# The mixing stage of a hybrid encoder layer, from tiles of 128 tokens to blocks of 384 tokens

## The chip, the core and the metric

The kernel runs on one core of a Trainium2 chip. The metric is the device time of one execution in microseconds (us). Engines are named as in the profile: PE (TensorE) multiplies matrices and transposes, DVE (VectorE), ACT (ScalarE) and POOL (GpSimd) do elementwise work, SP (SyncE) issues most transfers. PSUM is the memory that PE writes, SBUF the one that all engines read.

## The reference

One layer over 2048 prompt tokens and 64 sample tokens with 1024 channels. In short:

```python
mod = silu(c) @ w_ada + b_ada                     # sh1, sc1, g1, sh2, sc2, g2
h = x * (1 + sc1) + sh1
proj = h @ w_in                                   # q 512, k 128, v 128, a 512, g 512 columns
attn = sink_attention(q, k, v, bias, sinks)       # 8 heads, 2 kv heads, a window of 128 tokens and the own chunk
u = a * sigmoid(g)
y = depthwise_conv(u, w_dw, 31 taps) + b_dw       # 512 channels, causal
conv = silu(layer_norm(y))
mix = concat([attn, conv]) @ w_out
x1 = layer_norm(ALPHA * x + (1 + g1) * mix)
h2 = x1 * (1 + sc2) + sh2                         # goes on to a mixture of experts: 16 experts, 2 per token
```

The outputs are y for both sequences and the last keys, values and convolution inputs of each.

## The kernel before

Four stages follow one another, with a barrier between: `setup` (modulation vectors, weights split in two half-precision parts), `mix` (all of the above up to h2 and the router's logits), `route` with `experts`, and `finish`. The change is in `mix`, with small parts of `setup`.

`mix` works in 17 tiles: tile 0 holds the 64 sample tokens, tiles 1 to 16 hold 128 prompt tokens each. Every engine has its own program, written by hand, and runs it in order; engines meet at semaphores only. A step of the loop holds four tiles at different ages: the next tile's x (lag -1), projections of tile j0, attention and taps of j1, layer norm of the convolution and output projection of j2, residual and second modulation of j3. Steps 4 to 15 run in a hardware loop of two steps.

- Projections (L1110): tokens lie on PE's output partitions. For each of four jobs (q, k with v, g, a) 24 matmuls stream up to 512 columns of `w_in` past a stationary slice of `hT` (three products of half-precision parts, eight slices of 128 channels). The results lie token by token, so q, k and the gated input u are turned by PE transposes (`turn_in`, L1093) and copied by ACT.
- Modulation of x: two POOL operations over 1024 columns (L721, L723), then PE transposes, an ACT cast (L921) and a DVE subtraction (L1082) for the two parts of `hT`.
- Taps (L965): 31 taps over four channel groups, 124 DVE operations of 128 columns a tile, which read `uT` and add to `y`, both in SBUF. They are put between DVE's other work at fixed cuts (`TAP_CUTS`).
- Attention: scores in four rounds of two heads (L1124), DVE adds the bias and takes row maxima (L981), ACT takes exponentials head by head (L871), PE transposes them (p), ACT copies (L902), PE multiplies with v (L1184), ACT scales (L931), PE transposes (o).
- Convolution's norm: PE transposes y, DVE statistics (L991), POOL's power (L730), a DVE shift (L1002), ACT (L814), PE transposes back (z), ACT (L833, L837), DVE (L1033), ACT and POOL for the two parts.
- Output projection (48 matmuls of 512 columns), ACT copies (L806), POOL gate and residual (L740, L743), DVE statistics (L1017), shift (L1028), ACT normalizes (L848), POOL (L757 to L765), PE transposes h2, ACT copies (L887), router logits (L1168).

Of the kernel before, what the change touches and what calls it, by code (L numbers as in the profile page):

```python
# [20 lines left out]
F32 = mybir.dt.float32  # L21
# [6 lines left out]
P = 128  # L28
# [108 lines left out]
def build(nc, a):  # L137
# [3 lines left out]
    vec_rows = nc.dram_tensor("vec_rows", [6, 2, D], F32)  # L141
    bias_rows = nc.dram_tensor("bias_rows", [HEADS, NREL], F32)

    with ExitStack() as keep:
# [16 lines left out]
        with ExitStack() as mixer:  # L161
            def held(name, shape, dt=F32):
# [12 lines left out]
                "kT": held("kT", [P, 2, 2 * P]),  # L175
                "kv": held("kv", [P, 2, 2 * P]),
                "vprev": held("vprev", [P, 2, P]),
                "uT": held("uT", [P, 2, CB, HIST + P]),
# [33 lines left out]
def setup(nc, a, K, M, vec_rows, bias_rows):  # L212
    with ExitStack() as ctx:
# [23 lines left out]
        vec = sb("vec", [P, 6, 2, KD])  # L237
        onesc = sb("onesc", [P, 2, KD])
        vec_row = sb("vec_row", [96, P])
# [43 lines left out]

        pieces = [(a["w_in"][0, k * P:(k + 1) * P, :], [w[:, k, :] for w in M["w_in"]], INW) for k in range(KD)]
        pieces += [(a["w_out"][0, k * P:(k + 1) * P, :], [w[:, k, :] for w in M["w_out"]], D) for k in range(KD)]

        with nc.Block() as block:
# [22 lines left out]
            def _(pool):  # L310
# [7 lines left out]
                pool.memset(M["uT"][:, 1, :, 0:HIST], 0.0).then_inc(zeroed, 1)  # L318
# [8 lines left out]
            def _(act):  # L327
                for dst, src in ((dw_rows[:], a["w_dw"][0]), (cache_k[:], a["cache_attn_k"].rearrange("l b t h d -> (l b t) (h d)")),
# [3 lines left out]
                                 (M["vprev"][:, 0, :], a["cache_attn_v"].rearrange("l b t h d -> (l b t) (h d)"))):  # L332
# [19 lines left out]
                act.copy(M["kT"][:, 0, 0:P], ps_u[:, 0, :]).then_inc(history_ready, 1)  # L352
                act.wait_ge(history_turned, 2)
                act.copy(M["uT"][:, 0, :, 0:HIST], ps_b[:, 0:CB * HIST].rearrange("p (c t) -> p c t", c=CB)).then_inc(history_ready, 1)
                act.wait_ge(dw_turned, 1)
                act.copy(M["w_dw"][:], ps_t[:, :, 0:TAPS]).then_inc(dw_ready, 1)
# [10 lines left out]
                for i, (_, (hi, _), cols) in enumerate(pieces):  # L367
                    act.wait_ge(raw_loaded[i % RAW_RING], 16 * (i // RAW_RING + 1))
                    act.activation(hi, raw[:, i % RAW_RING, :cols], ACT.Copy, scale=W_SCALE).then_inc(hi_ready, 1)
# [6 lines left out]
                act.copy(vec_row[:], ps_v[0:96, :]).then_inc(vec_row_ready, 1)  # L376
# [7 lines left out]
            def _(pe):  # L384
# [41 lines left out]
                pe.transpose(ps_v[0:96, :], vec[:].rearrange("p v s k -> p (v s k)"), K["ident"][:]).then_inc(vec_turned, 1)  # L426

            @block.vector
            def _(dve):
# [9 lines left out]
                for c in range(ADA_CHUNKS):  # L439

                    while split < min(len(pieces), SPLITS_PER_CHUNK * (c - 2)):
                        _, (hi, lo), cols = pieces[split]
                        dve.wait_ge(hi_ready, split + 1)
                        dve.scalar_tensor_tensor(lo, raw[:, split % RAW_RING, :cols], W_SCALE, hi, ALU.mult, ALU.subtract).then_inc(lo_ready, 1)
# [13 lines left out]
                dve.tensor_scalar(vec[:, 0], part(1), 1.0, None, ALU.add).then_inc(vec_ready, 1)  # L458
                dve.tensor_copy(vec[:, 1], part(0)).then_inc(vec_ready, 1)
                dve.tensor_scalar(vec[:, 2], part(2), 1.0, 1.0 / (ALPHA * W_SCALE), ALU.add, ALU.mult).then_inc(vec_ready, 1)  # L460
                dve.tensor_scalar(vec[:, 5], part(5), 1.0, 1.0 / ALPHA, ALU.add, ALU.mult).then_inc(vec_ready, 1)
                dve.tensor_scalar(onesc[:], part(4), 1.0, None, ALU.add).then_inc(vec_ready, 1)
                dve.wait_ge(vec_ready, 5)
                dve.tensor_tensor(vec[:, 3], onesc[:], col(LN1_G), ALU.mult).then_inc(vec_ready, 1)
                dve.tensor_tensor(vec[:, 4], onesc[:], col(LN1_B), ALU.mult).then_inc(vec_ready, 1)
                dve.wait_ge(vec_ready, 7)
                dve.tensor_tensor(vec[:, 4], vec[:, 4], part(3), ALU.add).then_inc(vec_ready, 1)
# [8 lines left out]
TURNS = [("y", 0, 2), ("z", 0, 2), ("q", 0, 0), ("k", 0, 0), ("h2", 0, 3), ("h2", 1, 3),  # L476
         ("p", 0, 1), ("p", 1, 1), ("p", 2, 1), ("p", 3, 1), ("u", 0, 0), ("x", 0, -1), ("x", 1, -1), ("o", 0, 1)]

OUTPUTS = [("lg", 0, 3), ("pv", 0, 1), ("out", 0, 2), ("out", 1, 2)]


def before(ring, i, name, n):

    at = [(x, y) for x, y, _ in ring].index((name, n))
    m, c = i
    while True:
        at -= 2
        if at < 0:
            at += len(ring)
            c -= 1  # L490
            if isinstance(m, int) and c < -1:
                return None
        what, number, lag = ring[at]
        j = lagged((m, c), lag)
        if j is not None:
            return what, number, j


def mix(nc, a, K, M, vec_rows, hidden2, normed1):
    with ExitStack() as ctx:  # L500
# [7 lines left out]
        x_h = sb("x_h", [P, 2, D])  # L508
        x_res = sb("x_res", [P, D])
        rows = sb("rows", [P, 5, D])  # L510
        ln1_rows = sb("ln1_rows", [P, 2, D])
        hT = [sb(f"hT_{part}", [P, KD, P], F16) for part in ("hi", "lo")]
        q_tok = sb("q_tok", [P, AW])
        gate = sb("gate", [P, CH])
        qT = sb("qT", [P, 2, GROUP, P])
        y = sb("y", [P, 2, CB, P])
        probs = sb("probs", [P, HEADS, 2 * P])
        pT = sb("pT", [P, 2, 2, 2, P])
        o_tok = sb("o_tok", [P, AW])
        mixT = [sb(f"mixT_{part}", [P, KD, P], F16) for part in ("hi", "lo")]  # L520
# [4 lines left out]
        u_out = sb("u_out", [P, CH])  # L525
# [3 lines left out]
        h2T = sb("h2T", [P, KD, P])  # L529
        row_max = sb("row_max", [P, HEADS])  # L530
# [15 lines left out]
        score = [ctx.enter_context(nc.psum_tensor(f"score{n}", [P, 2, 2 * P], F32)) for n in range(2)]  # L546
        outp = [ctx.enter_context(nc.psum_tensor(f"outp{n}", [P, 512], F32)) for n in range(2)]


        x_loaded = [sem(f"x_loaded{n}") for n in range(2)]  # L550
# [1409 lines left out]
```

## Time and profile before

| | |
|---|---|
| time, median of three runs | 1859.59 us (1857.54 to 1860.09) |
| span of the profiled execution | 1858.3 us |
| what the median has beside the span | 1.3 us |
| mixing stage, first x load to the first load of the next stage | 121.7 to 1167.1 us |
| DVE, PE, ACT, POOL busy, share of the span | 84%, 80%, 43%, 31% |
| mean granted TensorE clock | 0.876 |

The span runs from the first to the last instruction of the profiled execution; all positions are us from its start. A clock of 1.00 is 2.4 GHz and 0.50 is 1.2 GHz. The shares are over all four stages, so what binds the mixing stage is to be read in windows of that stage.

### The profile page before, as it was taken

The page shows a single profiled execution, that of the slowest core. Times are in us where ns is not written, and L with a number is a line of the kernel's source. Part 1 is how long each engine was busy: PE and PEld are TensorE (multiplying, and loading weights), DVE is VectorE, ACT ScalarE, POOL GpSimd, SP SyncE. Part 2 cuts the span into 40 slices and gives each one's busy share as a digit, 9 for nine tenths or more (in the row PEclk, how much of TensorE's full clock was granted, in tenths as well). Part 3 has the DMA queues.
Part 4 walks back from the last instruction along what each step waited for, and adds up shares of the span by engine and source line. Part 5 has one row for each costly group of instructions (what it writes and reads, how often), then busy time and mean ns, then how long its engine had stood idle before and what let it go on. Part 6 is the DMA issues. An engine that isn't in the chain of part 4 may idle for free. (4 is left out here: it accounts for less than half of the span.)

```text
span 1858.3 us, 26059 instructions
## 1 busy us (share of the span) xinstructions
PE 1479.8 (80%) x7082; PEld 819.7 (44%) x7082; DVE 1555.3 (84%) x3420; ACT 802.2 (43%) x1429; POOL 582.9 (31%) x422
## 2 busy tenths in 40 slices
PE   5958988778887888878988864369999999995664
PEld 1214545445454554545545442335554555552221
DVE  1415899999999999999999970769999999993887
ACT  1302332333323333233332331058888888882332
POOL 0012132344323443234432335011222222213775
PEclk9978889889988898888988866579999999997777
DMA  9961011011000110001100001856899333324774
GB/s 325 400 212 39 12 49 32 35 47 46 24 33 34 46 46 23 35 34 46 46 23 23 28 35 45 283 161 239 288 322 385 113 111 107 110 101 152 227 231 153
DMA packets 90720, 218.28 MB, mean 117 GB/s; under 512 B 8034, under 2 KB 42758, under 8 KB 88591
## 3 DMA queue, kind: packets, MB, share of 16 engines
q1 hardware_dynamic: 65554, 136.25, 21.0%
q0 software_dynamic: 11808, 43.00, 7.2%
q10 hardware_dynamic: 13277, 38.20, 5.4%
q14 instruction: 61, 0.50, 0.1%
q8 instruction: 20, 0.33, 0.1%
HBM read 165.90 MB, written 51.56 MB: 117 GB/s over the span
## 5 line engine op out<-in xcount | busy, mean ns | idle before, releaser
L965 DVE SCALAR_TENSOR_TENSOR y<-uT,w_dw_cols,y 128x128 f32<-128x128 f32 (+1 forms) x2040 | 738.8, 437 | 0.7
L1655 DVE SCALAR_TENSOR_TENSOR w_gate_up_lo<-w_gate_up_ring,w_gate_up_hi 128x2048 f16<-128x2048 f16 x96 | 219.4, 2287 | 25.3 <-ACT w_gate_up_hi L1580 24.9
L1580 ACT ACTIVATE w_gate_up_hi<-w_gate_up_ring 128x2048 f16 x96 | 182.8, 1906 | 59.5 <-SPq L1538 40.1
L1100 PE MATMUL proj<-w_in_hi,hT_hi 128*128 128x512 f16 (+3 forms) x544 | 200.9, 369 | 1.1 <-DVE hT_lo L1082 1.1
L1100 PE MATMUL proj<-w_in_lo,hT_hi 128*128 128x512 f16 (+3 forms) x544 | 199.7, 367 | 0.0
L1100 PE MATMUL proj<-w_in_hi,hT_lo 128*128 128x512 f16 (+3 forms) x544 | 198.7, 365 | 0.0
L730 POOL TENSOR_TENSOR y_small<-y_small,mhalf 128x1 f32<-128x1 f32 (+1 forms) x17 | 9.3, 549 | 515.3 <-DVE y_small L996 515.3
L1698 PE MATMUL ps_up<-w_gate_up_hi,slot_rowsT_hi 128*128 128x512 f16 x384 | 147.0, 383 | 18.9 <-DVE slot_rowsT_lo L1680 14.0
L1561 POOL COPY slot_index<-slot_token 128x1 int32 (+1 forms) x48 | 44.8, 934 | 351.5 <-PE eturn L1719 308.4
L1698 PE MATMUL ps_up<-w_gate_up_lo,slot_rowsT_hi 128*128 128x512 f16 x384 | 146.6, 382 | 0.0
L1698 PE MATMUL ps_up<-w_gate_up_hi,slot_rowsT_lo 128*128 128x512 f16 x384 | 146.6, 382 | 0.0
L1100 PE MATMUL outp<-w_out_hi,mixT_hi 128*128 128x512 f16 (+1 forms) x272 | 111.3, 409 | 2.5 <-DVE logits L1068 2.5
L1686 DVE SCALAR_TENSOR_TENSOR w_down_lo<-w_down_ring,w_down_hi 128x2048 f16<-128x2048 f16 x48 | 109.6, 2284 | 3.3 <-ACT w_down_hi L1631 2.5
L1100 PE MATMUL outp<-w_out_lo,mixT_hi 128*128 128x512 f16 (+1 forms) x272 | 109.7, 403 | 0.0
L1100 PE MATMUL outp<-w_out_hi,mixT_lo 128*128 128x512 f16 (+1 forms) x272 | 108.5, 399 | 0.0
L1922 PE MATMUL ps_v<-x,ident 128*128 128x512 f32 (+1 forms) x68 | 57.0, 934 | 50.7 <-ACT y_rows L1869 46.9
L1093 PE MATMUL turn<-ident,gate 128*128 128x128 f32 (+1 forms) x68 | 18.3, 422 | 96.8 <-DVE gate L1063 96.8
L1631 ACT ACTIVATE w_down_hi<-w_down_ring 128x2048 f16 x48 | 91.7, 1911 | 5.8 <-issue 3.8
L418 PE MATMUL ps_mod<-w_ada_ring,c_silu 128*2 128x512 f32 x192 | 87.4, 610 | 8.6 <-DVE c_silu L433 4.3
L902 ACT COPY pT<-turn 128x512 f32<-128x512 f32 x60 | 33.8, 587 | 128.5 <-PE turn L1093 128.5
L1093 PE MATMUL turn<-ident,h 128*128 128x128 f32 (+1 forms) x136 | 27.2, 366 | 74.9 <-POOL h L759 74.9
L871 ACT ACTIVATE probs<-probs,nmax 128x256 f32<-128x256 f32 (+2 forms) x136 | 65.9, 485 | 39.0 <-DVE nmax L1044 39.0
(254 smaller groups left out, 3118.1 us busy)
## 6 DMA issues: line engine op xcount, KB each, us to landing
w_ada_ring<-in_w_ada SPq DMA_DIRECT2D x12, 2048.0 KB, 15.0
expert_rows<-out_rows ACTq DMA_DIRECT2D x48, 512.0 KB
w_gate_up_ring<-in_w_gate SPq DMA_DIRECT2D x16, 1024.0 KB
w_gate_up_ring<-in_w_up SPq DMA_DIRECT2D x16, 1024.0 KB
w_down_ring<-in_w_down SPq DMA_DIRECT2D x16, 1024.0 KB
x_h<-in_x_prompt SPq DMA_DIRECT2D x16, 512.0 KB
x_res<-in_x_prompt SPq DMA_DIRECT2D x16, 512.0 KB, 3.3
hidden<-h SPq DMA_DIRECT2D x16, 512.0 KB, 2.6
```

The costliest lines, as they stand in the source:

```text
L418: mm = pe.matmul(ps_mod[c % 2][:], c_silu[:, k:16:KD], w_ada[:, c % ADA_RING, k, :], start=(k == 0), stop=(k == KD - 1))
L871: act.activation(probs[:n, h, lo:hi], probs[:n, h, lo:hi], ACT.Exp, bias=nmax[:n, h:h + 1], accum_out=prob_sum[:n, h:h + 1]).then_inc(prob ...
L965: dve.scalar_tensor_tensor(y[:, p, c, :n], u, w, y[:, p, c, :n], ALU.mult, ALU.add).then_inc(taps_done, 1)
L1093: mm = pe.transpose(bank[:nf, place, :np_], src, ident[:np_, :np_])
L1100: mm = pe.matmul(out, x[xp][:, k, :n], w[wp][:, k, cols], start=(k == 0 and wp == xp), stop=(k == KD - 1 and xp == 1))
L1561: pool.tensor_copy(index[:, c:c + 1], K["slot_token"][:, tile_at(j)]).then_inc(index_ready, 1)
L1580: act.activation(gate_up_parts[0][:, at, k:k + KD // 2, :, :].rearrange("p k a n -> p (k a n)"), w_gate_up[:, bass.ds(b, 1), k:k + KD // 2 ...
L1631: act.activation(down_parts[0][:, c, :, :].rearrange("p k n -> p (k n)"), w_down[:, bass.ds(b, 1), :, :].rearrange("p b k n -> p (b k n)") ...
L1655: dve.scalar_tensor_tensor(flat[1], w_gate_up[:, bass.ds(b, 1), k, :, :].rearrange("p b k a n -> p (b k a n)"), W_SCALE, flat[0], ALU.mult ...
L1686: dve.scalar_tensor_tensor(flat[1], w_down[:, bass.ds(b, 1), :, :].rearrange("p b k n -> p (b k n)"), W_SCALE, flat[0], ALU.mult, ALU.subt ...
L1698: mm = pe.matmul(out, x, w, start=(k == 0 and xp == wp), stop=(k == blocks - 1 and xp == 1))
L1922: pe.matmul(ps_v[p][h][:n, :], ident[:n, :n], x1[:n, p, cols], start=True, stop=False)
```

## The change

The 17 tiles are grouped in six blocks: tiles 0 to 2 (64 + 128 + 128 tokens), four blocks of three tiles (384 tokens), and tiles 15 and 16. The loop is over phases p; the code is written out in full (no hardware loop). Phase p projects block p, and then makes up to three steps: in each, tile i of block p goes through attention (`mine`), tile i of block p-1 through output projection and residual (`leaves`), tile i+1 of block p-1 through the convolution's norm (`then`), tile i-1 of block p-1 through h2 and logits (`last`), and tile i of block p+1 through modulation and transposes (`nxt`).

- Projections: the weight slice is stationary and `hT` streams, up to 384 columns. q, k, g and a come out by channels, 13 jobs of 24 matmuls; v keeps tokens on partitions (24 matmuls of 128 columns a tile). The transposes of q, k and u go, and their copies. The score banks and the projection banks are the same two.
- Modulation: `x_part` on ACT reads the transposed x in PSUM and applies scale and shift per channel, four operations of 128 columns for each half, then a cast; DVE subtracts (`x_low`). POOL's two operations go.
- Taps: one operation covers the block's 350, 384 or 256 columns and adds up in PSUM (`tap_sum`), two channel groups in turn; the last tap writes `y` to SBUF. 744 operations in all, against 2108.
- Scores: two rounds of four heads. Exponentials of four heads, then of the other four.
- `gate` also holds the modulated x, and `y_tok` also holds the attention's output.

```diff
+BLOCKS = [[0, 1, 2], [3, 4, 5], [6, 7, 8], [9, 10, 11], [12, 13, 14], [15, 16]]
+JOBS = ["k", "q0", "q1", "q2", "q3", "v", "g0", "a0", "g1", "a1", "g2", "a2", "g3", "a3"]
...
+                def x_part(t, h):
...
+                    for c in range(4):
+                        k = 4 * h + c
+                        last = act.activation(h32[:, c, :n], turn_bank("x", t, h)[:, c, :n], ACT.Identity,
+                                              scale=M["mod_in"][:, 0, seq_of(t), k:k + 1], bias=M["mod_in"][:, 1, seq_of(t), k:k + 1])
+                    last.then_inc(h32_ready, 1)
+                    act.wait_ge(h32_ready, 2 * t + h + 1)
+                    act.copy(hT[0][:, 4 * h:4 * h + 4, at:at + n], h32[:, :, :n]).then_inc(hT_hi_ready, 1)
...
+                        u, w = U[:, c, k:k + n], M["w_dw"][:, c, k:k + 1]
...
+                            dve.wait_ge(taps_done, TAP_OPS * b + m - 1)
...
+                            to = y[:, c, 0:n] if k == TAPS - 1 else tap_sum[e][:, 0:n]
+                            dve.scalar_tensor_tensor(to, u, w, tap_sum[e][:, 0:n], ALU.mult, ALU.add).then_inc(taps_done, 1)
...
+                        at = {"k": K0, "q": Q0, "a": A0, "g": G0}[job[0]] + (int(job[1]) * P if len(job) == 2 else 0)
+                        for k in range(KD):
+                            for xp, wp in ((0, 0), (1, 0), (0, 1)):
+                                mm = pe.matmul(bank[:, 0:size(b)], M["w_in"][wp][:, k, at:at + P], hT[xp][:, k, 0:size(b)],
+                                               start=(k == 0 and xp == wp), stop=(k == KD - 1 and wp == 1))
...
+                        if mine is not None:
+                            scores(mine, 0)
+                        if then is not None:
+                            y_turn(then)
+                        if leaves is not None:
+                            out_project(leaves, 0)
+                        if then is not None:
+                            z_turn(then)
+                        if mine is not None:
+                            scores(mine, 1)
+                        if leaves is not None:
+                            out_project(leaves, 1)
+                        if last is not None:
+                            h2_turn(last)
+                        if mine is not None:
+                            prob_turn(mine, 0)
+                        if last is not None:
+                            logits(last)
...
+                        if mine is not None:
+                            attend(mine, 3)
+                            o_turn(mine)
```

ACT's order in a step is: norm of y (`then`), first half of the output copy (`leaves`), gain of the convolution (`then`), exponentials of four heads, high part of the convolution, second output copy, the other four exponentials, h2 copies (`last`), two copies of probabilities, `x_part` of the first half (`nxt`), two copies of probabilities, `x_part` of the second half, the residual's norm (`leaves`), the scaling of the attention's output (`mine`), its high part. On DVE the shift for the residual's norm stands behind `x_low` of the second half.

How the order moves shows best at two places. The first is PE in the middle of a step. `turn` are the transposes (probs: probabilities, o_tok or y_tok: the attention's output, x_h: the next x), `outp<-kv,pT` or `outp<-v,pT` the product with the values, and the router's logits stand ahead of it. Before, at the join of two steps of the loop:

```order
L1100 MATMUL outp<-w_out_hi,mixT_lo 128x512
L632 REGISTER_ALU
L1093 MATMUL turn<-ident,o_tok 128x128 x4
L1093 MATMUL turn<-ident,y 128x128 x4
L1118 REGISTER_ALU
L1124 MATMUL score<-kT,qT 128x256 x4
```

After, from the logits of one tile to the scores of the next:

```order
L1445 MATMUL outp<-w_router,h2T 128x20 x8
L1348 MATMUL turn<-ident,probs 128x128 x4
L1464 MATMUL outp<-v,pT 128x64 x4
L1348 MATMUL turn<-ident,x_h 128x128 x4
L1348 MATMUL turn<-ident,probs 128x128 x4
L1464 MATMUL outp<-v,pT 128x64 x4
L1348 MATMUL turn<-ident,probs 128x128 x4
L1464 MATMUL outp<-v,pT 128x64 x4
L1348 MATMUL turn<-ident,x_h 128x128 x4
L1464 MATMUL outp<-v,pT 128x64 x4
L1348 MATMUL turn<-ident,y_tok 128x128 x4
L1407 MATMUL proj<-kT,qT 128x256 x4
```

The transposes of the attention's output stood behind the output projection of another tile (48 matmuls); now they stand directly behind the attention that they belong to, and the scores of the next tile behind them.

The second place is DVE where one phase ends and the next begins. Before, the gated input of a tile (`gate<-gate,proj`) came between taps of 128 columns:

```order
L965 SCALAR_TENSOR_TENSOR y<-uT,w_dw_cols,y 128x128
L1061 REGISTER_ALU
L1062 REGISTER_ALU
L1063 SCALAR_TENSOR_TENSOR gate<-gate,proj 128x512
L1068 ISA
L1068 TENSOR_TENSOR logits<-outp,b_router 128x20
L964 REGISTER_ALU
L965 SCALAR_TENSOR_TENSOR y<-uT,w_dw_cols,y 128x128
```

After, from the last operation of a phase (`oT_lo`) to the next block's gated input (`uT<-gate,proj`):

```order
L1241 TENSOR_TENSOR oT_lo<-turn,oT_hi 128x512
L1155 SCALAR_TENSOR_TENSOR tap_sum<-uT,w_dw_cols,tap_sum 128x384 x9
L1262 TENSOR_TENSOR logits<-outp,b_router 128x20
L1155 SCALAR_TENSOR_TENSOR tap_sum<-uT,w_dw_cols,tap_sum 128x384 x38
L1155 SCALAR_TENSOR_TENSOR y<-uT,w_dw_cols,tap_sum 128x384 x2
L1165 COPY uT<-uT 128x2x30
L1173 SCALAR_TENSOR_TENSOR uT<-gate,proj 128x384
L1185 BN_STATS y_stat<-turn 128x6
```

Nine taps, the logits of the tile that leaves last, and 40 more taps stand ahead of the next block's first gated input and of the transposes of y.

## Rows read from the trace of the kernel before

**Rows 1.** Windows view, the loop's steps: length, then busy us and instructions by engine
```profile
core 0: us, PE busy (x) PEld busy (x) DVE busy (x) ACT busy (x) POOL busy (x), PEclk, DMA share, GB/s
211.00:1111.00 900.00, 737.58 (x3984) 461.43 (x3981) 874.07 (x2497) 301.88 (x829) 333.22 (x195) 0.89 0.10 35
```
**Rows 2.** Timeline of POOL, the power, once a tile: start us, duration us, engine
```profile
604.30 0.55 POOL L730 TENSOR_TENSOR y_small<-y_small,mhalf 128x1 f32<-128x1 f32 x1 [29.25 <-DVE y_small L996]
...
720.89 0.55 POOL L730 TENSOR_TENSOR y_small<-y_small,mhalf 128x1 f32<-128x1 f32 x1 [29.25 <-DVE y_small L996]
```
**Rows 3.** Timelines of DVE and POOL: taps alone and beside POOL, operations beside POOL
```profile
202.12 9.53 DVE L965 SCALAR_TENSOR_TENSOR y<-uT,w_dw_cols,y 128x128 f32<-128x128 f32 x36
...
604.81 2.49 POOL L740 TENSOR_TENSOR v<-v,rows 128x512 f32<-128x512 f32 x2
605.09 1.01 DVE L1002 SCALAR_TENSOR_TENSOR y_small<-y_aggr,y_small 128x1 f32<-128x1 f32 x1
606.02 0.68 DVE L1007 TENSOR_TENSOR mixT_lo<-turn,mixT_hi 128x512 f16<-128x512 f32 x1
...
619.43 2.35 POOL L759 TENSOR_TENSOR h<-h,rows 128x1024 f32<-128x1024 f32 x1
619.50 18.94 DVE L965 SCALAR_TENSOR_TENSOR y<-uT,w_dw_cols,y 128x128 f32<-128x128 f32 x28
```
**Rows 4.** Timeline of DVE: taps of 64 columns, operations of 512 columns
```profile
180.47 5.56 DVE L965 SCALAR_TENSOR_TENSOR y<-uT,w_dw_cols,y 128x64 f32<-128x64 f32 x28
...
614.35 0.68 DVE L1033 SCALAR_TENSOR_TENSOR conv<-y_tok,conv 128x512 f32<-128x512 f32 x1
...
643.06 0.68 DVE L1063 SCALAR_TENSOR_TENSOR gate<-gate,proj 128x512 f32<-128x512 f32 x1
```
**Rows 5.** Timeline of PE at full clock, one tile
```profile
601.77 1.99 PE L1124 MATMUL score<-kT,qT 64*128 64x256 f32 x8
...
605.00 0.38 PE L1100 MATMUL proj<-w_in_hi,hT_hi 128*128 128x512 f16 x1
605.21 0.38 PE L1100 MATMUL proj<-w_in_lo,hT_hi 128*128 128x512 f16 x1
...
629.63 1.86 PE L1168 MATMUL outp<-w_router,h2T 128*128 128x20 f32 x16
631.34 1.07 PE L1093 MATMUL turn<-ident,probs 128*128 128x128 f32 x8
...
634.20 0.39 PE L1184 MATMUL outp<-kv,pT 128*128 128x64 f32 x2
634.42 0.39 PE L1184 MATMUL outp<-vprev,pT 128*128 128x64 f32 x2
```
**Rows 6.** Timeline of ACT, one tile; the last row by groups: busy us, mean ns
```profile
609.58 1.50 ACT L833 ACTIVATE conv<-turn,cols 128x128 f32<-128x128 f32 x4
...
614.60 1.24 ACT L848 ACTIVATE n<-v,l_small 128x1024 f32<-128x1024 f32 x1 [2.08 <-DVE l_small L1028]
...
623.93 1.04 ACT L887 COPY h2T<-turn 128x512 f32<-128x512 f32 x2
...
647.24 1.75 ACT L931 ACTIVATE o_tok<-outp,rden 128x64 f32<-128x64 f32 x8
...
L871 ACT ACTIVATE probs<-probs,nmax 128x256 f32<-128x256 f32 x120 | 59.3, 495 | 37.1 <-DVE nmax L1044 37.1
```
**Rows 7.** Groups of DVE by line and form: busy us, mean ns
```profile
L981 DVE CUSTOM_DVE_ANT_0 probs<-score,bias 128x256 f32<-128x256 f32 x120 | 44.5, 416 | 3.5 <-issue 3.3
...
L1017 DVE BATCH_NORM_STATS2 l_stat<-v 128x6 f32<-128x512 f32 x32 | 20.4, 676 | 20.8 <-POOL v L743 20.8
```
**Rows 8.** Windows view, PE alone: length, busy us, granted clock
```profile
619.90:621.90 2.00, 0.06 (x1) 1.00 0.00 0
622.90:626.20 3.30, 3.30 (x10) 0.50 0.31 127
637.30:643.80 6.50, 0.00 (x1) 0.70 0.00 1
```
**Rows 9.** Timeline of SP: the first load of the mixing stage, the next stage's first
```profile
121.73 0.58 SPq L654 DMA_DIRECT2D x_h<-in_x_sample  x1
...
1167.10 0.66 SPq L1227 DMA_DIRECT2D w_gate_up_ring<-in_w_gate  x1
```

More of the change, by code:

```diff
@@ L470, in setup @@
         nc.clear_and_free_semaphores(sems)
         nc.all_engine_barrier()
[L476 to L496, printed above, removed]
+BLOCKS = [[0, 1, 2], [3, 4, 5], [6, 7, 8], [9, 10, 11], [12, 13, 14], [15, 16]]
@@ new lines, with out_order @@
+TURNS = turn_order()
+TURN_AT = {use: n for n, use in enumerate(TURNS)}
+def out_order():
+    order = []
+    for p in range(NB + 1):
+        if left_from(p) is not None:
+            order.append(("lg", left_from(p), 0))
+        for i in range(steps_of(p)):
+            mine, leaves, last = (tile_in(*x) for x in ((p, i), (p - 1, i), (p - 1, i - 1)))
+            if leaves is not None:
+                order += [("out", leaves, 0), ("out", leaves, 1)]
+            if last is not None:
+                order.append(("lg", last, 0))
+            if mine is not None:
+                order.append(("pv", mine, 1))
+    order.append(("lg", BLOCKS[-1][-1], 0))
+    return order
@@ new lines, in o_high @@
+                def o_high(t):
+                    n, b, i = width(t), BLOCK_OF[t], BLOCKS[BLOCK_OF[t]].index(t)
+                    act.wait_ge(o_turned, t + 1)
+                    older = tile_in(b - 1, i)
+                    if older is not None:
+                        act.wait_ge(out_done, 2 * older + 2)
+                    act.copy(oT[0][:, i, :, :n], turn_bank("o", t)[:, :, :n]).then_inc(oT_hi_ready, 1)
+                for t in BLOCKS[0]:
+                    for h in range(2):
+                        x_part(t, h)
@@ new lines, in wait_bank, with x_turn @@
+                def wait_bank(name, t, n):
+                    use = next(banks)
+                    assert use == (name, t, n), (use, name, t, n)
+                    if held[n] is not None:
+                        what, t_, n_ = held[n]
+                        s, value = out_read[what]
+                        pe.wait_ge(s, value(t_, n_))
+                    held[n] = use
+                def x_turn(t, h):
+                    n = width(t)
+                    pe.wait_ge(x_loaded, 16 * t + 16)
+                    turn_in("x", t, h, [(c, x_h[:n, (4 * h + c) * P:(4 * h + c + 1) * P], n, P) for c in range(4)], x_turned)
@@ L1216, in _, with h2_turn @@
-                over_steps(pe, step, first=-1)
+                            x = oT[xp][:, i, k, :n] if k < CB else convT[xp][:, t % 2, k - CB, :n]
+                            mm = pe.matmul(outp[h][:n, :], x, M["w_out"][wp][:, k, h * 512:(h + 1) * 512],
+                                           start=(k == 0 and xp == wp), stop=(k == KD - 1 and xp == 1))
+                    mm.then_inc(out_done, 1)
+                def h2_turn(t):
+                    n = width(t)
+                    pe.wait_ge(h2_ready, 2 * t + 2)
+                    for h in range(2):
+                        turn_in("h2", t, h, [(c, h2[:n, (4 * h + c) * P:(4 * h + c + 1) * P], n, P) for c in range(4)], h2_turned)
@@ L1219, in load_expert @@
+                h2_turn(BLOCKS[-1][-1])
+                logits(BLOCKS[-1][-1])
+                k_turn(BLOCKS[-1][-1])
+                state_turn(1)
 def load_expert(sp, a, W, e, b):
```

1309 lines of the change are left out of this document (757 added, 552 removed).

## The prediction

> **What bounds the kernel now.** First the windows of the mixing stage: in 900 us of its steps DVE is busy 874, PE 738, ACT 302, POOL 333 [rows 1]. DVE has no room, so its work sets the period, which POOL's once-a-tile power shows: 116.6 us for two tiles, 58.3 a tile, 174.9 for three [rows 2]. Then DVE's timeline says why. 36 taps that nothing disturbs take 9.53 us, 0.264 each; 28 taps beside POOL's long operations take 18.94, 0.676 each [rows 3]. A DVE operation that reads two SBUF tensors waits for POOL: the shift L1002, over one column, took 1.01 us, and ended when POOL's first half of L740 did; L1007, with one input in PSUM, ran beside POOL in 0.68 [rows 3]. Of 58.3 us a tile, 124 taps take 33 undisturbed and some 11 are lost beside POOL. PE's own work is less, so it waits for DVE, and its clock falls after each wait [rows 8].
>
> **What the change takes away.** 2108 taps become 744. From 64 to 128 columns a tap grows from 0.199 (5.56 by 28) to 0.264 [rows 3, 4], 1.02 ns a column, so 384 columns make 0.264 + 256 x 0.00102 = 0.525 us, and 256 make 0.395. No row shows DVE writing PSUM. The bounds are 0.39 (384 columns at that slope, no start-up) and 0.80 (a tap that lasts as long as a 512-column operation, 0.68, with the start-up of 0.13 that is left of a tap of 64 columns); I take 0.525, since a 512-column operation takes 0.68 with both inputs in SBUF and 0.68 with one in PSUM [rows 4]. The Trainium skill ("VectorE: DVE Perf Modes", section on the TRN2 errata) gives an operation from PSUM 62 cycles more than one from SBUF; by that a tap would be 0.59 and the whole 13 us longer. The two rows of 0.68 show no such difference, and the sum goes by them. The new taps have one SBUF input and so should not wait for POOL, as L1007 did not. Per block of three tiles DVE's taps fall from 3 x 44 = 132 us to 124 x 0.525 = 65. That takes DVE off the end of the chain. So the question is what is late next.
>
> **What is late next: the order inside a step.** PE runs in order. In a step it waits at the transposes of the attention's output for ACT, and only then starts the next tile's scores. Head and tail of a tile's attention therefore lie behind one another, where before another tile's output projection lay between. I follow the middle step of a block, at full clock, from the scores of its tile (time 0):
>
> Head: scores 2.0 [rows 5], y transposes 0.5, 24 matmuls of 0.215 = 5.2 [rows 5], to 7.7. DVE meanwhile: row maxima 4 x 0.37 = 1.5 [rows 7], statistics 1.3, two taps; its shift waits for POOL's multiply as L1002 did, to 7.9. ACT's norm 0.8, z transposes to 9.6, second scores to 11.6, row maxima and their maximum to 13.8.
> Tail: four exponentials of 0.494 (59.3 by 120) [rows 6] to 15.8, convolution cast 0.5; the second output projection ends at 16.8, its copy at 17.5; four exponentials and the sink to 19.6; two h2 copies 1.04 [rows 6] to 20.7; logits 1.86 [rows 5] to 22.7; probabilities' transposes 0.55, values 4 matmuls 0.9, x transposes 0.55 [rows 5] to 24.7; `x_part` 1.50 (as L833) + 0.1 + 0.6 = 2.2 [rows 6] to 27.0; two copies to 28.1, values and x transposes to 29.3; second `x_part` to 31.5; DVE's `x_low` 0.7 and shift 0.2, because the shift stands behind it, to 32.5; residual's norm 1.24 to 33.7; eight scalings 1.75 [rows 6] to 35.5; transposes to 36.1.
> POOL is not last here (residual done at 22.7, statistics of 2 x 0.64 [rows 7] at 24.4). The first step has no h2 and logits, 33.3; the third no y and z, 33.9. Together 103.3 us, of which PE works about 26 a step.
>
> **Projections.** A job is 24 x 0.215 x 384/512 = 3.87 us [rows 5]. Thirteen make 50.3. v's 72 matmuls of 128 columns are bounded by 0.054 (their columns alone) and 0.116 (a weight load and a short matmul, as the logits: 1.86 by 16 [rows 5]); I take 0.116, 8.4. Transposes and logits of the leaving tile make 4.0. The logits come after four jobs and the h2 transposes, at 18.5; 40 taps stand behind them on DVE, 21.0, to 39.7, and only then can PE turn y, which it reaches at 38.5. Another 0.6 for the last gated input. Sum 64.5 us.
>
> **Clock.** After 1.94 us of idle PE the granted clock was 0.50 from 622.9 to 626.2 though PE was busy, and it had fallen within 6.5 idle us [rows 8]. A stretch of 3.3 us at half clock costs 1.7. I put 1.7 on each of the three 5 us waits at the ends of steps, and half of it on the three shorter ones: 7.6 a block.
>
> A block of three tiles is 64.5 + 103.3 + 7.6 = 175.4, against 174.9 now. Steady state gains nothing.
>
> **The ends.** The stage lasts 1045.4 us now [rows 9]. After: first phase 140 (an estimate: three loads with `x_part` and `x_low`, 24; projection of 320 columns 50; three steps without another tile's work, 23, 20 and 23); block 1 171 (no logits beside its projections); blocks 2 to 4 3 x 175.4 = 526; the last block, 256 columns, 53 + 65 = 118; then 112 in which little overlaps (tile 14's residual and logits 32, 40 taps of 0.395 16, norm of tile 15 10, output projection 12, residual 10, POOL's modulation and residual of tile 16 15, norm and POOL's four operations 14, store 3); barrier 3. Sum 1070, 24 more than now. The transposes that go (nine of 53 a tile) and POOL's two operations are not on this path. Setup's split of `w_in` into more pieces lies beside the loads of `w_ada` there; if it doesn't, under 3 us. The later stages are the same. The sum is against the profiled execution, 1858.3 of span; the median has 1.3 beside that, which I keep. Forecast: 1859.6 + 24 = **1883 us**, for itself 1860 to 1910.
>
> **Rivals.**
> 1. The clock holds. PE's waits are shorter than I reckon, or fall so that the clock stays at 1.00. Then 7.6 a block and some in the ends go, 42 in all: 1841. For it: the dense projections; against: [rows 8], where 1.94 us of idle was enough. This is the rival on the other side; it decides once less than half of the clock's charge comes.
> 2. Scores overlap. In each new round consecutive score matmuls use different halves of the partitions, before the same half. If two of them run side by side, a round is 1.0 instead of 2.0 [rows 5] and 2 us go from each of some 14 full steps: 1855. The Trainium skill ("TensorEngine Tiling (Array Packing)", Tiling Modes) says that separate row tiles work in parallel, up to twice as fast. No run here shows it.
> 3. Taps are dear. At 0.80 DVE's 40 taps end 11 later in each of five phases, and the taps inside a step hold the second row maxima by 1 to 2: 1883 + 55 + 20 = 1958; at 0.66 half of that, 1920.
> 4. The waits hide one another and a step is PE's 26 us. Then 25 a block go: 1765. Against it stands the one order of PE, in which nothing lies behind the output's transposes.
>
> **How the numbers follow.** Chances: forecast 0.50, clock 0.17, scores 0.13, taps 0.14, PE-bound 0.06. About 0.2% (3.7 us) is what a measurement of this kernel can tell from no change. Faster comes from the clock (0.14 of 0.17), half of the scores' case (0.07), PE-bound (0.06) and the forecast's edge (0.06): 0.33; no change 0.08; slower 0.59. The range for 8 in 10 is 1825 to 1925: it takes in both clock cases and a tap of 0.66, and leaves out the PE-bound case and the dearest taps.
>
> **What would show it.** Right: in the new trace DVE is busy under 75% of the mixing stage; taps of 384 columns start 0.50 to 0.56 apart, also beside POOL; a step lasts 33 to 40 us; PE waits 4 to 6 us for the scaling of the attention's output at the end of each; ACT is busy nearly throughout the last 20 us of a step; the clock shows 0.50 at the start of steps. Wrong: steps under 31 us, or DVE busy throughout, or taps above 0.65, or a stage whose third block is far from 175 us.

## The result and the profile after

The changed kernel takes 1866.29 us (median of five runs, 1864.19 to 1866.97) against 1859.55 for the kernel before in the same session: 1.0038 of it, 95% interval 1.0025 to 1.0050. It is slower by 6.7 us, where 24 were forecast. The direction came out; the size of the change does not fit, so a term of the sum is wrong, and the experiments look for it.

The page of the profiled execution, its span and its busy times:

```profile
span 1863.6 us, 23581 instructions
PE 1454.6 (78%) x7587; PEld 856.5 (46%) x7587; DVE 1175.0 (63%) x2093; ACT 833.0 (45%) x1512; POOL 484.7 (26%) x388
```

DVE was 84% busy and is 63%; PE and ACT hardly moved. The windows view by phases answers to [rows 1] (length, then busy us and instructions of PE, weight loads, DVE, ACT and POOL, the granted clock, DMA):

```profile
121.30:270.50 149.20, 94.15 (x618) 69.77 (x619) 57.04 (x157) 51.33 (x167) 0.00 (x0) 0.69 0.14 44
270.50:436.20 165.70, 141.79 (x830) 94.96 (x828) 94.64 (x231) 61.71 (x167) 42.38 (x31) 0.84 0.10 32
...
609.20:779.90 170.70, 139.97 (x854) 93.19 (x852) 96.85 (x232) 63.61 (x169) 49.78 (x34) 0.88 0.10 38
...
947.90:1064.10 116.20, 95.28 (x666) 74.43 (x664) 69.59 (x182) 38.22 (x103) 33.20 (x25) 0.85 0.09 33
```

A full block takes 170.7 us where three tiles took 174.9 [rows 2], with DVE busy 97 of them. So the steady state did gain 4 us a block; the ends lost more. The stage lasts from 121.34 to 1175.56, 1054.2 us against 1045.4 [rows 9].

Timelines of DVE and of POOL beside it (start us, us, engine, line; x is the count) answer to [rows 3]:

```profile
629.00 20.04 DVE L1155 SCALAR_TENSOR_TENSOR tap_sum<-uT,w_dw_cols,tap_sum 128x384 f32<-128x384 f32 x38
715.25 2.34 POOL L863 TENSOR_TENSOR n<-n,rows 128x1024 f32<-128x1024 f32 x1
715.62 1.99 DVE L1195 SCALAR_TENSOR_TENSOR y_small<-y_aggr,y_small 128x1 f32<-128x1 f32 x1
717.53 2.71 DVE L1155 SCALAR_TENSOR_TENSOR tap_sum<-uT,w_dw_cols,tap_sum 128x384 f32<-128x384 f32 x5
717.67 2.36 POOL L865 TENSOR_TENSOR n<-n,rows 128x1024 f32<-128x1024 f32 x1
```

38 taps take 20.04, 0.527 each; five beside POOL's L865 take 2.71, 0.54 each (a tap's own record is 0.62 long and overlaps the next one, which weighs more in a group of five). No tap of the whole kernel has a record of over 0.623. L1195, over one column with both inputs in SBUF, begins beside POOL's L863 and ends with it, after 1.99 us. The taps, which now have one input in PSUM, are not held up by POOL, as the prediction reckoned from L1007.

PE's middle step of that block, from one tile's transposes of the attention's output (`turn<-ident,y_tok`) to the next tile's (in brackets the wait and its releaser), answers to [rows 5]:

```profile
708.64 1.11 PE L1348 MATMUL turn<-ident,y_tok 128*128 128x128 f32 x4 [4.35 <-ACT y_tok L1050]
709.69 2.08 PE L1407 MATMUL proj<-kT,qT 64*128 64x256 f32 x8
...
719.24 1.13 PE L1407 MATMUL proj<-kT,qT 64*128 64x256 f32 x8
...
728.97 0.63 PE L1348 MATMUL turn<-ident,probs 128*128 128x128 f32 x4 [2.43 <-ACT h2T L1017]
729.43 1.89 PE L1445 MATMUL outp<-w_router,h2T 128*128 128x20 f32 x16
...
744.61 1.12 PE L1348 MATMUL turn<-ident,y_tok 128*128 128x128 f32 x4 [5.11 <-ACT y_tok L1050]
```

The step is 36.0 us long (708.64 to 744.61), as forecast at full clock (36.1), but not in the way it was forecast: the second round of scores takes 1.13 us, not 2.0. The first takes 2.08, at half clock. The windows view of PE alone, around the start of that step (length, busy, clock), answers to [rows 8]:

```profile
704.30:708.60 4.30, 0.00 (x0) 0.50 0.26 101
708.60:714.40 5.80, 5.76 (x21) 0.50 0.22 90
714.40:718.70 4.30, 4.30 (x21) 0.99 0.00 2
```

Behind the wait of 4.35 us the clock stays at 0.50 through 5.8 us of work; the 3.3 us of [rows 8] stood behind 1.9 us of idle. It did not fall in that wait, though: it shows 0.50 from the wait's first microsecond. The fall came earlier in the step, while PE worked, some 2 us behind a shorter wait of 2.34 us. PE's timeline, and the windows view with the columns of the phases above:

```profile
695.60 1.10 PE L1464 MATMUL outp<-v,pT 128*128 128x64 f32 x8 [2.34 <-ACT pT L1027]
```

```profile
690.00:695.00 5.00, 3.26 (x20) 1.81 (x17) 2.93 (x6) 4.16 (x18) 3.34 (x3) 1.00 0.00 0
695.00:700.00 5.00, 4.40 (x29) 4.21 (x29) 2.04 (x7) 3.63 (x9) 3.05 (x4) 0.74 0.24 66
700.00:705.00 5.00, 4.30 (x21) 4.11 (x20) 1.61 (x4) 2.71 (x6) 0.21 (x1) 0.50 0.33 112
```

The view of PE's waits over the mixing stage (us, times, the longest):

```profile
PE turn L1348 <- ACT y_tok L1050: 67.0, 17, 5.1
PE turn L1348 <- DVE y L1155: 27.3, 4, 10.7
PE turn L1348 <- ACT h2T L1017: 21.9, 9, 2.5
PE outp L1464 <- ACT pT L1027: 15.0, 11, 2.3
```

The first row is the wait at the ends of steps. The second is the wait of the transposes of y for the 40 taps that stand behind the logits; another 16 us of the same kind lie in the drain.

### The profile page after: what moved, and what is told of

Its sections match the earlier page's. It is cut to its first block and busy times, and to the rows that moved or that the text cites. A ratio compares the mean times of both kernels' runs of the same rounds, so it can differ in the third digit from the quotient of the medians.

```text
span 1863.6 us, 23581 instructions
## 1 busy us (share of the span) xinstructions
PE 1454.6 (78%) x7587; PEld 856.5 (46%) x7587; DVE 1175.0 (63%) x2093; ACT 833.0 (45%) x1512; POOL 484.7 (26%) x388
## 5 line engine op out<-in xcount | busy, mean ns | idle before, releaser
L1155 DVE SCALAR_TENSOR_TENSOR tap_sum<-uT,w_dw_cols,tap_sum 128x384 f32<-128x384 f32 (+2 forms) x696 | 356.0, 589 | 0.0
L1918 ACT ACTIVATE w_gate_up_hi<-w_gate_up_ring 128x2048 f16 x96 | 182.8, 1906 | 59.9 <-SPq L1876 40.1
L1391 PE MATMUL proj<-hT_hi,w_in_hi 128*128 128x384 f16 (+2 forms) x624 | 201.8, 323 | 5.5 <-DVE hT_lo L1180 5.5
L1391 PE MATMUL proj<-hT_lo,w_in_hi 128*128 128x384 f16 (+2 forms) x624 | 201.2, 322 | 0.0
L1391 PE MATMUL proj<-hT_hi,w_in_lo 128*128 128x384 f16 (+2 forms) x624 | 201.1, 322 | 0.0
L1464 PE MATMUL outp<-v,pT 128*128 128x64 f32 (+2 forms) x528 | 99.4, 351 | 17.9 <-ACT pT L1027 15.0
L1464 PEld LDWEIGHTS outp<-v,pT 128*128 128x128 f32 (+2 forms) x528 | 94.9, 268 | 24.5 <-ACT pT L1027 18.4
L1180 DVE TENSOR_TENSOR hT_lo<-gate,hT_hi 128x512 f16<-128x512 f32 (+1 forms) x34 | 22.9, 672 | 111.1 <-ACT hT_hi L909 111.1
L1348 PE MATMUL turn<-ident,y_tok 128*128 128x128 f32 (+1 forms) x136 | 29.0, 352 | 76.8 <-ACT y_tok L1050 67.0
L1247 DVE BATCH_NORM_STATS2 l_stat<-v 128x6 f32<-128x512 f32 (+1 forms) x34 | 21.9, 685 | 99.8 <-POOL v L839 99.8
L1348 PE MATMUL turn<-ident,probs 128*128 128x128 f32 (+2 forms) x264 | 54.4, 348 | 36.0 <-ACT h2T L1017 21.9
```

The source lines that it names most:

```text
L1155: dve.scalar_tensor_tensor(to, u, w, tap_sum[e][:, 0:n], ALU.mult, ALU.add).then_inc(taps_done, 1)
L1348: mm = pe.transpose(bank[:nf, at, :np_], src, ident[:np_, :np_])
L1391: mm = pe.matmul(bank[:, 0:size(b)], M["w_in"][wp][:, k, at:at + P], hT[xp][:, k, 0:size(b)], start=(k == 0 and xp == wp), stop=(k == KD - ...
L1464: mm = pe.matmul(outp[1][:n, h * HD:(h + 1) * HD], pT[:nk, f % 2, e, kt, :n], V[:nk, slot, s * HD:(s + 1) * HD], start=(x == 0), stop=(x = ...
L1918: act.activation(gate_up_parts[0][:, at, k:k + KD // 2, :, :].rearrange("p k a n -> p (k a n)"), w_gate_up[:, bass.ds(b, 1), k:k + KD // 2 ...
```

## The experiments

Every time is a median beside the kernel before on the same chip (1859.4 to 1860.3 there). "The changed kernel" is 1866.3.

### Is a round of scores short because its matmuls alternate halves?

```diff
-                    for e in range(2):
-                        for s in range(KV):
+                    for s in range(KV):
+                        for e in range(2):
```

> The four score matmuls of a round go in pairs on the same half of the partitions instead of alternating halves; nothing else changes. Theory A (two consecutive score matmuls on different halves run side by side, and the forecast priced them one behind the other): a round grows from 1.07 to 2.0 us at full clock and from 2.08 to about 4 at half clock; one to three us go on each of some 14 full steps, 1866 + 14 to 40 = 1880 to 1906 us. Rival B (the forecast only charged too much for the clock, and rounds last what they last): rounds stay at 1.07 and 2.08, 1862 to 1870 us.

Measured 1869.8 us (ratio to before 1.0058, 1.0038 to 1.0078). PE's timeline, a second round:

```profile
713.50 1.14 PE L1407 MATMUL proj<-kT,qT 64*128 64x256 f32 x8
```

Rival B's numbers, but they do not show its reason: in the records of single instructions they begin in pairs, some 10 ns apart, in this order as well, although four instructions of one half stand ahead of four of the other in the program. So this run did not separate the theories. The round must be put on one half.

### The scores on one half

```diff
-                            mm = pe.matmul(score[s][:n, e, lo:hi], qT[s * HD:(s + 1) * HD, 2 * r + e, at:at + n],
-                                           KT[s * HD:(s + 1) * HD, at + lo:at + hi], start=True, stop=True)
+                    for e in range(GROUP):
+                        mm = pe.matmul(score[e // 2][:n, e % 2, lo:hi], qT[r * HD:(r + 1) * HD, e, at:at + n],
+                                       KT[r * HD:(r + 1) * HD, at + lo:at + hi], start=True, stop=True)
```

> All four heads of a round of scores lie on one half of the partitions (the first round takes the four heads of the first half, the second round the others; DVE's row maxima follow). In the run that only changed the order inside a round, eight instructions still took 1.14 us and began in pairs 10 ns apart; in the kernel before, where eight in a row lie on one half, they began 0.215 apart and took 1.99. Theory A (halves run side by side, whatever the order, and the forecast priced a round at 1.99 by the kernel before): a round takes 2.0 at full clock and some 4 at half clock; 1 to 2.9 us of it a step on the path, 1866 + 17 to 45 = 1883 to 1911 us. Rival B (the rounds are short for another reason): 1.07 as now, 1862 to 1870. Rival C (rounds grow, but lie beside the chain of the convolution's norm): 2.0 and 4.0, and 1866 to 1876.

Measured 1909.6 us (1.0273, 1.0259 to 1.0287): 43.3 more than the changed kernel. PE's timeline, first and second round of one step, and PE's windows around its start:

```profile
724.24 1.11 PE L1348 MATMUL turn<-ident,y_tok 128*128 128x128 f32 x4 [5.11 <-ACT y_tok L1050]
725.28 3.78 PE L1406 MATMUL proj<-kT,qT 64*128 64x256 f32 x8
...
736.61 1.99 PE L1406 MATMUL proj<-kT,qT 64*128 64x256 f32 x8
```

```profile
719.20:724.20 5.00, 0.00 (x0) 0.75 0.32 107
724.20:731.70 7.50, 7.46 (x21) 0.50 0.17 70
731.70:736.60 4.90, 4.90 (x25) 0.98 0.01 2
```

Theory A. On one half a round takes 1.99 at full clock, to the hundredth what [rows 5] has, and 3.78 at half clock; on both halves 1.13 and 2.08. In this run and in the last one, a round writes its two PSUM banks in the same order; only the halves differ, so it is the half and not the bank. A block is 181.8 us long (first scores at 692.9 and 874.6), 11.1 more than in the changed kernel (676.8 and 847.5). This is also the kernel that the forecast priced, and it is 26.6 us above the forecast: something else was priced too low.

### What the half clock costs

```diff
                     n = width(t)
+                    if 3 <= t <= 14:
+                        pe.wait_ge(scores_used, 2 * t + 2)
+                        for k in range(20):
+                            pe.matmul(proj[0][:, :], hT[0][:, 0, 0:P], M["w_in"][0][:, 0, 0:512], start=True, stop=True)
                     pe.wait_ge(o_ready, t + 1)
```

First without the line on t, that is in all tiles:

> 20 matmuls of 512 columns (0.215 each, 4.3 us) into a free bank of PSUM stand ahead of the transposes of the attention's output, so that PE is busy while it waits for ACT's scaling; their result is overwritten. If the half clock at the start of a step is on the path, as the forecast charged it with 1.7 us a step: the clock stays at 1.00, transposes 1.11 to 0.55, first scores 2.08 to 1.07, 1866 - 17 x 1.7 = 1837 us, at most 1830. Rival: the half clock lies beside the chain of the convolution's norm (POOL's power behind its modulation), and only the transposes' 0.55 is on the path: 1866 - 17 x 0.55 = 1857 us. If the filler only delays the transposes: 1866 to 1875.

Measured 1863.2 (1.0011, 0.9995 to 1.0026): no clear gain. The starts of the scores show two effects that nearly cancel: a block of three went from 170.7 to 167.0 us, but two steps of the first block and one of the last grew by 3.5, 1.7 and 3.4, since their waits are shorter than the filler. Hence the version for tiles 3 to 14:

> The 20 filler matmuls in the changed kernel, in tiles 3 to 14 only (the first try had them in every tile, where the first and last blocks have shorter waits and lost some 12 us). By the steps of the first try a block of three tiles gains 3.7 us: 1866 - 15 = 1851 us. By the forecast's charge of 1.7 at the end of each step: 1866 - 20 = 1846. If the clock is not on the path: 1863 to 1869.

Measured 1852.7 (0.9967, 0.9953 to 0.9981): 13.6 less than the changed kernel, 1.1 a step. PE's timeline shows the wait filled and both operations behind it at full clock:

```profile
685.38 4.48 PE L1473 MATMUL proj<-w_in_hi,hT_hi 128*128 128x512 f16 x20
690.65 0.66 PE L1348 MATMUL turn<-ident,y_tok 128*128 128x128 f32 x4 [0.79 <-ACT y_tok L1050]
691.23 1.13 PE L1407 MATMUL proj<-kT,qT 64*128 64x256 f32 x8
```

And the same filler with the scores on one half:

> Scores on one half of the partitions, as in the run of 1909.6 us, and 20 filler matmuls ahead of the transposes of the attention's output in tiles 3 to 14 (the filler's result is overwritten). With scores as dear as the forecast priced them a block took 181.7 us, 6.3 more than the 175.4 forecast; its half clock lasts from the transposes to 7.4 us later, and the first round takes 3.78. If the clock after the wait is what the forecast priced too low: the first round falls to 2.0, a block to 168 to 172 us, 1910 - 4 x 10 to 14 = 1854 to 1870 us. If the clock was priced rightly (1.7 a step): 1910 - 12 x 1.7 = 1889 us. If something else makes the block long: 1900 to 1910.

Measured 1875.7 (1.0087, 1.0073 to 1.0101), between the first two expectations: 33.9 less than without filler, 2.8 a step. A block is 171.0 us (677.8 to 848.8). The four runs side by side:

| us | without filler | filler in tiles 3 to 14 | what the clock costs, in net |
|---|---|---|---|
| scores on one half | 1909.6 | 1875.7 | 33.9 |
| scores on both halves | 1866.3 | 1852.7 | 13.6 |
| what one half costs | 43.3 | 23.0 | |

Both costs are net, since the filler also moves the half clock. In the third block with both halves it stays at 1.00 where it fell at some 697 in the changed kernel, ahead of the filled wait, and the transposes behind that wait come 1.3 us sooner after the tile's first scores (30.5 against 31.8). In the next step the logits (710.27) now take 3.44 us, at half clock, instead of 1.89, and from the second scores to the transposes it is 27.7 us instead of 25.4.

Each cost depends on the other, since a first round on one half runs at half clock, where it is 1.8 longer than at full clock (3.78 against 1.99) and one on both halves 0.95 (2.08 against 1.13). In the changed kernel not all of it is on the path: 5.8 us at half clock are worth 2.9, but from the transposes to the second scores it is 9.0 us with the filler and 10.6 without, as PE then waits 0.95 for ACT's norm of y. Behind the wait the half clock lasts 7.5 us of work with the scores on one half and 5.8 in the changed kernel; in the one it fell within the wait, in the other ahead of it. Why was not tried.

### The order inside a step

PE's transposes of the attention's output move behind the next tile's scores, transposes of y and half of the output projection (at the end of a block: behind the first job); `o_low` moves with them. PE's part:

```diff
                             out_project(leaves, 0)
+                        if late is not None:
+                            o_turn(late)
+                            late = None
                         if then is not None:
                             z_turn(then)
...
                             attend(mine, 3)
-                            o_turn(mine)
+                            late = mine
```

> The transposes of the attention's output move on PE behind the next tile's first scores, the transposes of y and the first half of the output projection (at the end of a block: behind the first projection job); DVE's low part moves with them. If the order inside a step sets the period, as the forecast says: PE no longer stands idle for 4 to 5 us at the end of a step, the clock stays up there, and a middle step falls from 36 to 29 to 34 us, 14 steps 1866 - 28 to 98 = 1768 to 1838 us. Where POOL's power (behind the modulation of another tile) holds the norm of y as before, only some 2 us a step, 1838. Rival: ACT's work sets the step in any order, 1858 to 1870 us.

Measured 1826.8 (0.9820, 0.9800 to 0.9840), 39.5 less. PE's waits:

```profile
PE turn L1364 <- DVE y L1164: 43.3, 5, 15.9
PE turn L1364 <- ACT h2T L1026: 29.9, 9, 4.4
PE turn L1364 <- ACT y_tok L971: 24.2, 11, 4.8
```

The 67 us of waiting for the scaling are gone (2.2 left), and 17 us come back ahead of the z transposes (L971, the norm of y, 6.9 in the changed kernel), 8 at the copies of h2 and 8 at the projections, which wait 13.7 for the low part of x (5.5 in the changed kernel). The 43.3 contain the 16 of the drain. The wait at the end of a step was a matter of order, as the prediction said.

### The taps behind the logits

```diff
-                        more(6)
+                        more(12)
...
-                        more(2)
+                        more(5)
                         if nxt is not None:
                             x_low(nxt, 1)
                         if leaves is not None:
                             l_shift(leaves)
-                        more(2)
+                        more(7)
```

> 14 more taps in each step, at three places where DVE stands idle for 2.5 to 4.8 us, so that 7 instead of 49 taps are left for the next block's projections. If the 40 taps behind the logits set when y can be transposed, as the forecast reckoned (1.2 us of wait; the trace shows 27 us in four blocks and 16 in the drain): the wait goes, 1866 - 27 to 43 = 1823 to 1839 us. Rival: the taps delay row maxima and statistics inside the steps by as much as they save, 1855 to 1875 us.

Measured 1826.2 (0.9815, 0.9796 to 0.9833), 40.1 less. The group of y's transposes (busy us, mean ns, idle before them and its releaser):

```profile
L1348 PE MATMUL turn<-ident,y 128*128 128x128 f32 (+1 forms) x68 | 13.6, 334 | 3.0 <-DVE y L1155 3.0
```

43.3 us of waiting in five places became 3.0. The middle step took 14 more taps with a loss of 1 us (36.0 to 37.1).

### Did DVE set the period before?

Fifteen taps instead of 31 in the kernel before:

```diff
-        TAP_OPS = TAPS * CB
+        TAP_OPS = 15 * CB
...
-        TAP_CUTS = (10, 12, 13, 15, 22, 26, 28)
+        TAP_CUTS = (5, 6, 6, 7, 11, 13, 14)
...
-                        taps(j1, TAP_CUTS[6], TAPS)
+                        taps(j1, TAP_CUTS[6], 15)
```

> The kernel before with 15 of the 31 taps (the other 16 are left out of the convolution). If DVE's work sets the period there, as the prediction read it, a tile falls from 58.3 us to what PE needs, about 49 by its 96.9 busy in 117 us, and 15 tiles give 1860 - 140 = 1720 us, 1700 to 1760. Rival (the order on PE and ACT sets it and DVE is only full): 1840 to 1860 us.

Measured 1696.1 (0.9118, 0.9106 to 0.9131). POOL's power, four times in three periods, and the windows view of that stretch:

```profile
574.67 0.55 POOL L730 TENSOR_TENSOR y_small<-y_small,mhalf 128x1 f32<-128x1 f32 x1 [21.63 <-DVE y_small L996]
...
718.08 0.55 POOL L730 TENSOR_TENSOR y_small<-y_small,mhalf 128x1 f32<-128x1 f32 x1 [21.57 <-DVE y_small L996]
```

```profile
574.67:718.08 143.41, 137.26 (x785) 87.87 (x784) 122.17 (x285) 58.64 (x160) 64.19 (x39) 0.96 0.12 44
```

A tile falls from 58.3 to 47.8 us, somewhat below the 49 expected, and PE is busy 96% of it. DVE did set the period. The old order, with half of the taps gone, does three tiles in 143.4 us; the new one takes 170.7 with DVE at 57%.

### A version that beats both

Both moves together:

> The later transposes of the attention's output and the 14 earlier taps a step, together. If the two waits are separate places (the end of a step; the transposes of y in the projections), the gains add up: 1866 - 40 - 40 = 1786 us, 1780 to 1800. If one gain is the other's (DVE is on the path of the shorter step): 1805 to 1826.

Measured 1779.2 (0.9559, 0.9546 to 0.9572): the two gains add up, and 7 us more. Then four moves at once: the transposes in the middle of that half of the output projection (`o_low` behind the shift of the norm of y), POOL's power first, the residual's shift first, and 10 more taps a step than the changed kernel has, in place of the 14. What each of the four gives was not tried apart. PE's and POOL's part:

```diff
-                            out_project(leaves, 0)
+                            out_project(leaves, 0, 0, CB)
                         if late is not None:
                             o_turn(late)
                             late = None
+                        if leaves is not None:
+                            out_project(leaves, 0, CB, KD)
...
-                        if last is not None:
-                            modulated(last)
                         if then is not None:
                             y_rstd(then)
                         if last is not None:
+                            modulated(last)
                             gained(last)
```

> The later transposes, put into the middle of the first half of the output projection; POOL's power ahead of its modulation; the shift of the residual's norm ahead of the second low part of x; 10 more taps a step. If the order inside a step is what is left: the norm of y comes some 2.5 us earlier than in the run with the later transposes alone, a middle step falls from 32.8 to 29 to 31 us, 1786 - 14 x 2 to 3 = 1745 to 1770 us. Rival: ACT's own work in the second half of a step holds the period, 1780 to 1800 us.

Measured 1762.4 (0.9477, 0.9463 to 0.9491). PE now waited 26.4 us in nine steps for ACT's copies of h2, so these went ahead of the second four exponentials:

```diff
-                        if mine is not None:
-                            exps(mine, range(4, 8))
                         if last is not None:
                             h2_copy(last)
+                        if mine is not None:
+                            exps(mine, range(4, 8))
```

> The version of 1762 us with ACT's two copies of h2 ahead of the second four exponentials. PE's next transposes of probabilities wait for these copies 2.4 to 3.4 us in nine steps, and the logits stand behind. If that wait is on the path: 9 to 14 steps lose 1.6 to 2 us, 1762 - 14 to 28 = 1734 to 1748 us. Rival (the copies of probabilities behind the last exponential hold the step): 1758 to 1766 us.

Measured 1732.7 (0.9319, 0.9301 to 0.9337), 127 us below the kernel before and 134 below the changed one. The windows view of one block of three:

```profile
616.60:763.40 146.80, 137.57 (x852) 92.93 (x853) 99.77 (x233) 63.32 (x169) 49.76 (x33) 0.91 0.12 44
```

146.8 us a block with the same work as in 170.7, PE busy 94%: the gain came from the order, with what the clock gives back when PE waits less (0.91 against 0.88).

## Why the prediction was right in direction and wrong in size

**What bound the kernel before**: right, by the run with 15 taps.

**DVE off the end of the chain**: right. Taps are 0.527 apart (0.525 forecast) and 0.54 beside POOL; DVE is busy 57% of the block. By the prediction's estimate from the Trainium skill ("VectorE: DVE Perf Modes", section on the TRN2 errata) a tap would take 0.59; the spacing of 0.527 in the trace does not agree, and the rows of 0.68 with and without PSUM were the better guide.

**The order inside a step is what is late next**: right. PE waits 4.4 to 5.1 us for the scaling at the ends of full steps (4 to 6 forecast), and moving the transposes took 39.5 us away. One sign that the prediction named did not come: ACT is busy for 12.9 of the last 20 us of the middle step (725.65 to 745.65), not nearly throughout. Its own terms for that stretch have ACT waiting for PE and DVE in turn, and so does the trace.

**The sum of a block**, third block, from the scores of its first tile to those of the next:

| us | forecast | measured | from |
|---|---|---|---|
| first, middle, third step | 33.3, 36.1, 33.9 | 32.9, 36.0, 34.2 | starts of the scores; end of the last transposes, 779.9 |
| projections | 64.5 | 67.6 | 779.9 to 847.5 |
| clock | 7.6 | within the above | |
| sum | 175.4 | 170.7 | |

Three errors stand in it. **The step that failed is the price of the scores, "scores 2.0 [rows 5]" and "second scores to 11.6".** The eight instructions of that row lie on one half of the partitions (in the code before, two rounds in a row have the same `s`), and the new rounds use both. A round is 1.13 at full clock, and the whole is worth 43.3 us, shown by the run on one half. The prediction had this mechanism as its second rival, at 28 us and a chance of 0.13; it was the right one, and dearer than reckoned, since it also counts at half clock, where a first round saves 1.7.

**The clock** was at 0.50 behind the charged waits, as forecast, but the charge was 1.7 where the scores as priced cost 2.8 a step in net (33.9 by 12). With both halves it is 1.1. Without the charge for three step ends the forecast's block is 170.3, against 171.0 measured with filler and one half: as a sum the chain of operations was right within 1 us. That is in part luck, for the two errors of the next paragraph cancel in it, and the filled kernel still has half clock (its middle step's logits take 3.29 us). The charge at the step ends was 5.7 short in this block (10.8 recovered by the filler, 5.1 charged), and the scores 11.1 too long.

**The projections** held two errors that cancel. The 72 matmuls of v follow one another at 0.056, near the lower bound of 0.054, and make 4.0 instead of 8.4; the transposes of y wait 5.5 for the taps instead of 1.2. The 67.6 contains about 2.9 of half clock behind two waits.

**The ends**: first phase 149.2 (140 forecast), block 1 165.7 (171), blocks 2 to 4 173.0, 170.7 and 168.0 (175.4 each), last block 116.2 (118), then 111.5 to the next stage (115). In the first phase 26 us pass up to the first projection (24 forecast), the projections take 50 (50) and the three steps 73 (66); why its steps are longer was not tried. The later stages were 3.2 us shorter in this execution.

Put together: 1883, plus 26.6, is the 1909.6 measured with scores on one half; less 43.3 it is the 1866.3 of the changed kernel. In the trace of the one-half run the 26.6 can be placed (24.9 in that execution): the first phase takes 152.1 us there (140 forecast), block 1 169.0 (171), blocks 2 to 4 181.6, 181.7 and 175.6 (175.4 each), the last block 122.5 (118) and the rest 112.5 (115). So 12 of them lie in the first phase and 13 in the three full blocks. That the forecast was off by only 17 is owed to errors of opposite sign.

Of the other rivals, taps at 0.66 or 0.80 and a PE-bound step did not come; "the clock holds" did not come either: it showed 0.50 behind the waits, and even with the ends of the middle steps filled the time is 1875.7 with scores as priced and 1852.7 as they are, not 1841.

## What to carry to other kernels

A row prices a new operation only if its operands lie in the same places: here the matmul's shape was the same and the half of the partitions was not. When a change takes the bounding engine off the path and the time does not fall, look at the order on the engine that now waits: for each long wait ask what independent work could stand ahead of it, and test that before any operation is made faster. Filling a wait with dummy work shows what the clock behind it costs, but only in net: look in the trace whether the half clock has moved elsewhere, as it did here.

## What the runs showed of the hardware that was not expected

- Score matmuls on the two halves of the partitions run side by side in either program order: 1.13 and 1.14 us for eight against 1.99 on one half. The Trainium skill ("TensorEngine Tiling (Array Packing)", Tiling Modes) says that separate row tiles work in parallel; these runs agree, by a factor of 1.76.
- The DVE taps that add up in PSUM are not held up by POOL (0.54 against 0.527), while an operation of a single column with two SBUF inputs took 1.99 us beside it.
- With the scores on one half the clock fell within a wait of 5.1 us (0.75 over it) and stayed at 0.50 through 7.5 us of work. In the changed kernel it had fallen ahead of the wait of 4.35 us, some 2 us of work behind a wait of 2.3, and stayed at 0.50 through 5.8 us of work behind the longer one. With PE kept busy in the longer wait it showed 1.00 at both places of the changed kernel, and 0.50 in the logits of the step behind.
- Half-precision matmuls of 128 columns, each with a weight load of its own (the page counts as many loads as matmuls), follow one another at 0.056 us, 72 of them from 632.61 to 636.57. The first two in PE's timeline of the changed kernel:

```profile
632.61 0.22 PE L1385 MATMUL proj<-w_in_hi,hT_hi 128*128 128x128 f16 x1
632.66 0.22 PE L1385 MATMUL proj<-w_in_lo,hT_hi 128*128 128x128 f16 x1
```
